# Conditioning weights as contiguous pieces with a third of their sums on TensorE, the memory projected token-major, six tiles begun by halves

## The reference

```
mod = silu(c) @ w_ada + b_ada            # c: 2048 numbers, w_ada: 2048 x 6144
shift, scale, gate = split(mod, 3)
h = rms(x) * norm_g * (1 + scale) + shift
proj = h @ w_in                          # 64 output tiles of 128 columns
```

```
m_k, m_v = split(rms(mem) @ w_mem_kv, 2)   # 2048 x 1024
kc = rms over each head of m_k; vc = m_v
oc = softmax(qc kc^T / sqrt(128)) vc * silu(c_gate)
```

## Time and profile before

| | |
|---|---|
| median of three runs | 2829.59 us |
| profiled execution | 2827.68 us, its span 2826.4 us |
| TensorE busy | 96%, weight loads 78% |
| VectorE, ScalarE, GpSimd busy | 38%, 37%, 46% |
| granted TensorE clock, mean | 0.979 |
| DMA | 323 MB, mean 114 GB/s |
| tenths of TensorE busy, first 4 of 40 slices (70.7 us each) | 7, 4, 7, 9 |
| its clock in these | 9, 6, 7, 9 |
| GB/s in these | 345, 262, 172, 209 |
| chain that ended last | TensorE 85%, VectorE 7%, GpSimd 3%, DMA 2% |

### The profile page before, as it was taken

How to read it: one execution, slowest core, us unless ns; L and a number is a source line. 1 busy time by engine, 2 the same in 40 slices (tenths; PEclk the granted TensorE clock), 3 DMA queues, 4 the chain that set the end, 5 groups by cost and what they waited for, 6 DMA issues and landing times.

```text
span 2826.4 us, 31555 instructions
## 1 busy us (share of the span) xinstructions
PE 2724.9 (96%) x12512; PEld 2203.1 (78%) x12512; DVE 1065.4 (38%) x1699; ACT 1059.1 (37%) x1744; POOL 1287.2 (46%) x647
## 2 busy tenths in 40 slices
PE   7479999999999999999999999999999999999999
PEld 5467788887877878878888777777888888888787
DVE  7867744334212212134467333333222222222300
ACT  5123333343433433234443444444444444333311
POOL 5664333333433335453334434444545555655543
PEclk9679999999999999999999999999999999999999
DMA  9745422122222223432222223222233333333343
GB/s 345 262 172 209 155 69 75 69 74 78 86 86 83 86 86 127 143 129 82 77 77 86 83 87 99 93 90 89 101 101 114 103 115 109 123 116 116 127 145 108
DMA packets 102963, 323.29 MB, mean 114 GB/s; under 512 B 11425, under 2 KB 14497, under 8 KB 102305
## 3 DMA queue, kind: packets, MB, share of 16 engines
q1 hardware_dynamic: 99072, 307.64, 31.5%
q10 hardware_dynamic: 3744, 13.63, 1.4%
HBM read 304.45 MB, written 16.78 MB: 114 GB/s over the span
## 4 chain that ended last, share of the span: by engine, by line
PE 85%; DVE 7%; POOL 3%; DMA 2%; issue 2%; ACT 2%; SPq 0%; DVEq 0%; ACTq 0%; POOLq 0%
PE bank L647 25%; PE bank L649 24%; PE bank L648 24%; PE bank L889 2%; PE bank L877 2%; DVE TA L1383 2%; POOL wlo L1763 2%; PE bank L808 2%; DVE TA L1583 1%; PE bank L869 1%; DMA TA<-in_strip 1%; PE bank L736 1%; ACT whi L946 1%; DVE Y L1383 1%; PE bank L839 1%
## 5 line engine op out<-in xcount | busy, mean ns | idle before, releaser
L1763 POOL TENSOR_TENSOR wlo<-wraw,whi 128x1024 fp32r<-128x1024 f32 (+2 forms) x454 | 1061.6, 2339 | 1346.5 <-ACT whi L946 1346.4
L647 PE MATMUL bank<-Hhi,whi 128*128 128x512 f32 x2928 | 1202.8, 411 | 20.0 <-POOL Hlo L1784 9.8
L648 PE MATMUL bank<-Hlo,whi 128*128 128x512 f32 (+1 forms) x3056 | 1190.2, 389 | 0.0
L649 PE MATMUL bank<-Hhi,wlo 128*128 128x512 f32 x2928 | 1150.7, 393 | 0.0
L946 ACT ACTIVATE whi<-wraw 128x1024 fp32r<-128x1024 f32 (+2 forms) x454 | 456.8, 1007 | 696.7 <-PE bank L649 695.5
L647 PEld LDWEIGHTS bank<-Hhi,whi 128*128 128x128 f32 x2928 | 554.6, 189 | 164.3 <-issue 31.6
L648 PEld LDWEIGHTS bank<-Hlo,whi 128*128 128x128 f32 x3056 | 584.5, 191 | 122.3 <-issue 14.0
L649 PEld LDWEIGHTS bank<-Hhi,wlo 128*128 128x128 f32 x2928 | 554.1, 189 | 120.1
L1383 DVE SCALAR_TENSOR_TENSOR TA<-TA,par 128x1024 f32<-128x1024 f32 x60 | 127.4, 2124 | 10.1 <-DMA TA<-in_w_ada 4.4
L647 PE MATMUL bank<-Ohi,whi 128*128 128x512 f32 x320 | 128.8, 403 | 0.0
L649 PE MATMUL bank<-Ohi,wlo 128*128 128x512 f32 x320 | 124.9, 390 | 0.0
(11 more groups left out here) (237 smaller groups left out, 2592.6 us busy)
## 6 DMA issues: line engine op xcount, KB each, us to landing
wraw<-in_w_in SPq DMA_DIRECT2D x304, 512.0 KB, 3.2
TA<-in_w_ada SPq DMA_DIRECT2D x64, 512.0 KB, 4.8
Y<-in_w_ada SPq DMA_DIRECT2D x32, 512.0 KB, 3.9
wraw<-in_w_out SPq DMA_DIRECT2D x32, 512.0 KB, 3.2
wraw<-in_w_o SPq DMA_DIRECT2D x32, 512.0 KB, 3.2
wraw<-in_w_mem ACTq DMA_DIRECT2D x16, 512.0 KB, 5.5
tmp_mgs<-TA SPq DMA_DIRECT2D x32, 256.0 KB, 2.0
TA<-tmp_mgs SPq DMA_DIRECT2D x32, 256.0 KB, 3.5
```

The source lines that it names most:

```text
L647: e.matmul(out, hi[:, c], xhi[k], start=first and j == 0, stop=False)
L648: e.matmul(out, hi[:, c], xlo[k], start=False, stop=False)
L649: m = e.matmul(out, lo[:, c], xhi[k], start=False, stop=last and end)
L1763: e.tensor_tensor(M.wlo[b][:, 0:w], M.wraw[b][:, 0:w], M.whi[b][:, 0:w].bitcast(F32), ALU.subtract).then_inc(S.lo)
```

## The change

- **Conditioning weights.** w_ada is laid out as 96 blocks of 128 x 1024, each contiguous. Of the first 64 pieces every third (`by_tensor`: a % 3 == 2, 21 of them) is taken by TensorE, eight one-column fp32 matmuls straight from the landed piece into the PSUM columns of the totals; VectorE sums the other 43, into one accumulator a chunk (two in turn), whose eight totals matmuls are added to the same columns. Six places instead of four. SP issues all 64 loads in its setup, x's loads among them, the masks' at the 40th. The chunks' order stays (2, 0, 3, 1).
- **Memory.** w_mem as 16 items of 128 features x 1024 columns, one a k. The memory tile is the stationary operand (128 tokens), the weights are the moving one, 512 wide: 12 matmuls a k into four banks, kept open over all k. The norm over features is a column per token: two one-column matmuls a k. Keys and values come out token-major, so values need no transpose; keys are normed by ScalarE's square, a reduce and a multiplication on VectorE (`mem_kv`) and turned by eight transposes on TensorE. Only tiles 0 to 7 are prepared in setup, 8 to 15 in the loop, whose steps also hold: x's squares and sums (k below 8), x's norm (k = 8 to 11), the gain and h tiles 0 to 7, two a step (k = 12 to 15), three conditioning pieces in each. The pair of the memory tiles lies behind HIGH of h.
- **Begun tiles.** The six are begun in another order and in other banks. Before each of the first four stand four conditioning pieces; before the sixth the totals of chunks 3 and 1 and the making of h tiles 8 to 15. The masks' cast follows them.
- **Gates.** One piece in three slots (`GATE_SLOTS`) instead of in each.

```diff
-BEGUN = (40, 32, 48, 56, 41, 33)
+BEGUN = (48, 33, 40, 32, 56, 41)
+
+CHUNKS = (2, 0, 3, 1)
+PLACES = 6
...
+def by_tensor(a):
+
+    return a % 3 == 2
+
+
+def taken(a, tensor):
+
+    return sum(by_tensor(i) == tensor for i in range(a + 1))
...
     do["setup"]()
-    beat.add("core", do["x_norm"]())
-    beat.add("slow", do["condition"]((2, 0), 0))
-    for h in range(4):
-        full("mem", "mem_k", h)
-        full("mem", "mem_v", h)
-    beat.drain("post", "core", "slow")
-    do["h_prep"](0)
-    beat.add("slow", do["condition"]((3, 1), 2))
+    for k in range(KT):
+        do["mem"](k)
+    beat.add("core", do["mem_kv"]())
 
 
     begun = {}
-    for tile, bank in zip(BEGUN, (beat.open(), beat.open(), BS0, BS1, BT, BST)):
+    for n, (tile, bank) in enumerate(zip(BEGUN, (BS0, BST, beat.open(), beat.open(), BS1, BT))):
         begun[tile] = bank
-        do["part"]("h", range(8), bank, True, False)
-    beat.drain("slow")
-    do["h_prep"](1)
+        if n < 4:
+            do["ada"](range(48 + 4 * n, 52 + 4 * n))
+        if n == 5:
+            do["h_gain"](1)
+            do["h_put"](HIGH)
+        do["part"]("h", LOW, bank, True, False)
+    beat.drain("core")
+    do["masks"]()
     beat.add("slow", do["gates"]())
...
+    def mem(k):
+
+        i = beat.item
+        hi, lo = M.whi[i % NRING], M.wlo[i % NRING]
+        xhi, xlo = M.pair["mem"]
+        pe.wait_ge(S.msq, k + 1)
+        for tt in range(2):
+            m = e.matmul(M.bST[:, tt:tt + 1], M.mem_sq[k % 8][:, tt * P:(tt + 1) * P], ones[:, 0:1],
+                         start=k == 0 and tt == 0, stop=k == KT - 1, skip_group_check=True)
+        m.then_inc(S.mst)
+        pe.wait_ge(S.lo, i + 1)
+        pe.wait_ge(*ready["mem", k])
+        for kv in range(2):
+            w = slice(kv * T, (kv + 1) * T)
+            for tt in range(2):
+                c, out = slice(tt * P, (tt + 1) * P), M.banks[MEM_BANKS[2 * kv + tt]]
+                e.matmul(out, xhi[k][:, c], hi[:, w], start=k == 0, stop=False)
+                e.matmul(out, xlo[k][:, c], hi[:, w], start=False, stop=False)
+                m = e.matmul(out, xhi[k][:, c], lo[:, w], start=False, stop=k == KT - 1)
+        m.then_inc(S.item)
+        if k < 8:
+            for x in (2 * k, 2 * k + 1):
+                pe.wait_ge(S.xsq, x + 1)
+                e.matmul(M.bS0, ones, M.xsq[x % 4], start=x == 0, stop=x == KT - 1).then_inc(S.xst)
+        ada(range(3 * k, 3 * k + 3))
+        if k == 6:
+            totals(0)
+        if k == 11:
+            totals(1)
+        if k >= 12:
+            h_put((2 * k - 24, 2 * k - 23))
+        beat.done("mem", [])
+        if k == KT - 1:
+            free[BS0], free[BST] = (S.xr, 1), (S.rr, 1)
+            free.update({bank: (S.mkv, n + 1) for n, bank in enumerate(MEM_BANKS)})
+            free[BVV] = (S.adp, 2)
+
+    def ada(pieces):
+
+        for a in pieces:
+            if by_tensor(a):
+                half, c = a // 32, a // 16 % 2
+                pe.wait_ge(S.ada[a % PLACES], 16 * (a // PLACES + 1))
+                pe.wait_ge(S.setv, 8)
+                for i in range(8):
+                    at = 8 * c + i
+                    m = e.matmul((M.bV, M.bO)[half][:, at:at + 1], M.ada_slot[a % PLACES][:, i * P:(i + 1) * P],
+                                 M.par[:, 64 + a % 16:65 + a % 16], start=a in (2, 32) and i == 0, stop=False,
+                                 skip_group_check=True)
+                m.then_inc(S.adq)
+
+    def totals(chunk):
+
+        pe.wait_ge(S.adm, taken(16 * chunk + 15, False))
+        for i in range(8):
+            at = 8 * (chunk % 2) + i
+            m = e.matmul((M.bV, M.bO)[chunk // 2][:, at:at + 1], M.ada_acc[chunk % 2][:, i * P:(i + 1) * P],
+                         ones[:, 0:1], start=False, stop=True, skip_group_check=True)
+        m.then_inc(S.adc)
+
+    def h_gain(half):
+        totals(2)
+        totals(3)
...
+    def mem(k):
+        if k < 8:
+            mem_gain(k + 8)
+        ada(range(3 * k, 3 * k + 3))
+        if k < 8:
+            mem_rest(k + 8)
+        elif k < 12:
+            for x in (4 * k - 31, 4 * k - 29):
+                dve.wait_ge(S.xr, 2)
+                e.tensor_tensor(M.y[x], M.y[x], M.xr, ALU.mult).then_inc(S.xnv)
+        else:
+            if k == 12:
+                h_gain(0)
+            h_put((2 * k - 24, 2 * k - 23))
+        beat.done("mem", [])
+
+    def ada(pieces):
+
+        for a in pieces:
+            if not by_tensor(a):
+                chunk, c, done = a // 16, M.par[:, 64 + a % 16:65 + a % 16], n.up("adm") - 1
+                acc, src = M.ada_acc[chunk % 2], M.ada_slot[a % PLACES]
+                dve.wait_ge(S.ada[a % PLACES], 16 * (a // PLACES + 1))
+                dve.wait_ge(S.setv, 8)
+                if done == taken(16 * chunk - 1, False):
+                    dve.wait_ge(S.adc, chunk - 1)
+                    e.tensor_scalar(acc, src, c, None, ALU.mult).then_inc(S.adm)
+                else:
+                    dve.wait_ge(S.adm, done)
+                    e.scalar_tensor_tensor(out=acc, in0=src, scalar=c, in1=acc, op0=ALU.mult,
+                                           op1=ALU.add).then_inc(S.adm)
+
...
+        for a in range(4 * 16):
+            if a in (0, 2, 4, 6):
+                i = a // 2
+                e.dma_start(M.Y[:, i * 2048:(i + 1) * 2048], io["xT"][:, i * 2048:(i + 1) * 2048]).then_inc(S.x[i], 16)
+            if a == 40:
+                e.dma_start(M.masks_in.bitcast(I32), io["masks"]).then_inc(S.mask, 16)
+            if a >= PLACES:
+                sp.wait_ge(S.adq if by_tensor(a) else S.adm, taken(a - PLACES, by_tensor(a)))
+            e.dma_start(M.ada_slot[a % PLACES], io["w_ada"][CHUNKS[a // 16], a % 16]).then_inc(S.ada[a % PLACES], 16)
...
-        "w_ada": I["w_ada"][0], "w_in": tiles(I["w_in"][0]), "w_out": tiles(np.roll(I["w_out"][0], 1024, axis=0)),
-        "w_mem": tiles(I["w_mem_kv_2"][0]), "w_in2": w_in2, "w_kv": w_kv,
+        "w_ada": I["w_ada"][0].reshape(128, 16, 6, 1024).transpose(2, 1, 0, 3), "w_in": tiles(I["w_in"][0]), "w_out": tiles(np.roll(I["w_out"][0], 1024, axis=0)),
+        "w_mem": I["w_mem_kv_2"][0].reshape(16, 128, 1024), "w_in2": w_in2, "w_kv": w_kv,
```

More of the change, by code:

```diff
@@ L978, in setup, with square @@
         load(NRING)
+        act.wait_ge(S.setv, 9)
+    def square(k):
+        act.wait_ge(S.mem[k // 4], 16)
+        act.wait_ge(S.mst, k - 7)
+        e.activation(M.mem_sq[k % 8], M.memt[k], ACT.Square).then_inc(S.msq)
+    def mem(k):
+        split(beat.item + 2)
+        load(beat.item + 4)
+        if k < 8:
+            square(k + 8)
+            for x in (2 * k, 2 * k + 1):
+                act.wait_ge(S.x[x // 4], 16)
+                act.wait_ge(S.xst, x - 3)
+                e.activation(M.xsq[x % 4], M.y[x], ACT.Square).then_inc(S.xsq)
+            put("mem", k + 8, M.memt, k + 8, ("mg", k + 9), None)
+        if k == 8:
+            act.wait_ge(S.xst, KT)
+            e.activation(M.xr, M.bS0, ACT.Ln, scale=1.0 / D, bias=M.eps).then_inc(S.xr)
+            act.wait_ge(S.xr, 1)
+            e.activation(M.xr, M.xr, ACT.Exp, scale=-0.5).then_inc(S.xr)
+        if k >= 12:
+            h_put((2 * k - 24, 2 * k - 23))
+        beat.done("mem", [])
@@ new lines, in h_gain @@
+    def h_gain(half):
+        dve.wait_ge(S.adc, 2 * half + 2)
+        for c in range(2):
+            cc = CHUNKS[2 * half + c]
+            e.tensor_tensor(M.par[:, 8 * cc:8 * cc + 8], (M.bV, M.bO)[half][:, 8 * c:8 * c + 8],
+                            M.c("b_ada", 8 * cc, 8), ALU.add).then_inc(S.adp)
+            n.up("adp")
+        dve.wait_ge(S.adp, n["adp"])
+        c = slice(16 + 8 * half, 24 + 8 * half)
+        e.tensor_scalar(M.par[:, c], M.par[:, c], 1.0, None, ALU.add).then_inc(S.vstep)
+        n.up("vstep")
+        step()
+        e.tensor_tensor(M.par[:, c], M.par[:, c], M.c("norm_g", 8 * half, 8), ALU.mult).then_inc(S.vstep)
+        n.up("vstep")
@@ L1389, in totals, with gates @@
-    def totals(chunks):
-        dve.wait_ge(S.adt, n.up("adt"))
-        for c, cc in enumerate(chunks):
-            e.tensor_tensor(M.par[:, 8 * cc:8 * cc + 8], M.bV[:, 8 * c:8 * c + 8], M.c("b_ada", 8 * cc, 8),
+    def gates():
+        for g in range(2):
+            for j in range(16):
+                i, done, c = 16 * g + j, n.up("adm") - 1, M.par[:, 64 + j:65 + j]
+                dve.wait_ge(S.adg[i % 3], 16 * (i // 3 + 1))
+                if j == 0:
+                    dve.wait_ge(S.adc, 4 + g)
+                    e.tensor_scalar(M.gate_acc, M.gate_slot[i % 3], c, None, ALU.mult).then_inc(S.adm)
+                else:
+                    dve.wait_ge(S.adm, done)
+                    e.scalar_tensor_tensor(out=M.gate_acc, in0=M.gate_slot[i % 3], scalar=c, in1=M.gate_acc,
+                                           op0=ALU.mult, op1=ALU.add).then_inc(S.adm)
+                yield from rest(GATE_SLOTS)
+            dve.wait_ge(S.adc, 5 + g)
+            cc = 4 + g
```

(1 more changed line is left out.)

407 lines of the change are left out of this document (179 added, 228 removed).

## The result

The kernel with the change takes 2796.26 us (median of four runs, 2792.75 to 2800.78), the one before 2828.96 in the same series: a ratio of 0.9886, interval [0.9867, 0.9905]. That is 32.7 us faster; 41 were forecast (29+12). The profiled execution took 2796.65 us (span 2795.3), 31.1 less in its span than before.

The account below looks back on a forecast made before the run. TensorE was taken as the bound, busy 2724.9 of 2826.4 us, its loss lying at the head. From 2827.7 us, 29 for the anchor and 12 for the gates were subtracted: 2786.7, predicted as 2787, range 2764 to 2812.

Parts of the forecast that it names:

- the anchor: End of the first part with HIGH on TensorE: forecast at 188 us instead of 217, 29 us gained.
- Step 2: Memory loop, k=0 to 7: 6.6 us a step on TensorE, but loads of 25.6 MB at 346 GB/s set 74 us.
- Steps 3 and 4: Memory loop, k=8 to 11 and 12 to 15: VectorE sets the pace, 31 and 29 us.
- The rival with that factor: VectorE and GpSimd fully block each other: loop steps of 9.1 and 8.2 us, 9 us more, 2796; chance 0.14.
- The 30% idleness of TensorE: Sign for the memory loop: between 74 and 133 us TensorE is idle about 30%, VectorE under 5%.
- The lockstep rival: Memory loop: each step's waits drop TensorE's clock; at 1.2 GHz throughout the kernel is at 2855 us; chance 0.08.
- Step 5: Begun tiles, pieces and totals between the memory loop's end and the anchor: 55 us, with VectorE's work and loads covered.
- Step 6: Conditioning pieces as contiguous blocks: no gain taken, since load rates were equal at 349 GB/s.
- loads gain: Rival: 12% more load rate cuts Step 2 from 74 to 70 us, some later pieces sooner, 2782; chance 0.12.
- Step 7: Gates at one sum in three slots: 12 us gained, bounds all 26.3 us back or a loss of 10.
- the sum of 153.8 us: TensorE's priced work from 217.0 to 397.1 us, half tiles and three chains; it took 180.1, so 26.3 lost.
- the lower bound: Step 7's worst case: a loss of 10 us, 32 gate sums meeting later chain steps at 0.3 us.

Follow-up runs that it names:

- e3: The changed kernel with gate sums in each slot again instead of every third: 2812.75 us, ratio 0.9954 to the kernel before.
- e14: The kernel before the change with only its gate sums respaced, one piece in three slots: 2812.21 us, ratio 0.9956 to the kernel before.
- e4: The changed kernel with only the first of the eight one-column products made in each TensorE conditioning piece: 2784.78 us, ratio 0.9851 to the kernel before.
- e11: The changed kernel with each TensorE conditioning piece as two 512-wide products, silu(c) column held, sums unused: 2794.44 us, ratio 0.9889 to the kernel before.
- e2: The changed kernel with every second conditioning piece on TensorE instead of every third: 2824.83 us, ratio 0.9998 to the kernel before.
- e8: The changed kernel with all of x's normalisation on VectorE, none on GpSimd, and h's gains on ScalarE: 2794.18 us, ratio 0.9883 to the kernel before.
- e1: The changed kernel with all 64 conditioning pieces summed on VectorE, none on TensorE: 2802.89 us, ratio 0.9915 to the kernel before.
- e5: The changed kernel with w_ada in its old layout, pieces as strided slices instead of contiguous blocks: 2799.01 us, ratio 0.9903 to the kernel before.
- e10: The changed kernel with every fourth conditioning piece on TensorE instead of every third: 2794.32 us, ratio 0.9883 to the kernel before.
- e12: The changed kernel with e11's wide products, x's normalisation all on VectorE and h's gains on ScalarE: 2790.27 us, ratio 0.9874 to the kernel before.

## Why the prediction was right, and where its sizes were not

Faster by over 0.3% was right, and 2796 lies in the range. The forecast of 2787 missed by 9.7 us, as two misses of opposite sign: 13 too much at the anchor, 3 to 5 too little for the gates (15.4 and 17.4 in the traces of e3 and e14).

**Step 2, 6 us short, and for another reason.** Step 7 was to end at 74 us by the loads; it ended at 80.1. Steps 0 to 2 take 9.6, 9.0 and 9.3 us instead of 6.6: the loads are full there, TensorE waits 2.6 us in all, and its clock is 0.81 and 0.82 in steps 1 and 2. From 43 us to the end of the loop TensorE waits for nothing and sets the pace itself: 6.7 us a step as priced, 8.5 in step 6 with the totals that I had left out, 8.3 in step 7 at clock 0.79. The loads' 346 GB/s of the earlier trace rows was what was asked for, not what could be had: 415 was measured above, and the kernel before itself moved 383 from 10 to 43 us. At 415 the 25.6 MB take 62 us. That TensorE sets the pace from 43 us on is shown by e4.

**Steps 3 and 4, right in size.** VectorE begins step 8's sums at 76.1 us and ends step 15 at 138.8, 62.7 us later (61 forecast with the root of x): 33.2 us for the four steps of normalisation (32), 29.5 for the four of gains (29). From 74 to 133 us it is idle 7.6% of the time (under 5% forecast). The sums cost 2.28 us beside GpSimd, as in the earlier trace rows. The price that I had a little too low is the normalisation, 1.87 us instead of 0.61+0.75x1.36 = 1.63. Counted as in the prediction, by GpSimd's prices alone (8x2.40+8x1.36 = 30.1 us, an estimate), 13 sums and 8 normalisations were slowed by 13x1.00+8x1.26 = 23 us, a factor of 0.77; beside GpSimd's busy 37.7 us it is 0.61. The Trainium skill's exclusive lock ("SBUF — State Buffer", section "SBUF: two separate sides") asks for a factor of 1; here it is below 1 by either count, so it again agrees in kind only. The rival with that factor forecast 2796, the measured time, but by chance: its steps were to take 9.1 and 8.2 us, and they took 8.3 and 7.4.

**The 30% idleness of TensorE, wrong.** From 43 to 133 us it is never idle. It fills the time by running slower: 0.82, then 0.72. From 80 to 133 us the mean is 0.77, and 53.0x0.77 = 41 us is what eight steps of 4.9 us and one totals of 1.8 cost at full clock: the 12 us between are the idleness that I had forecast. I had tied a low clock to waits, and took the four one-column groups of a step for harmless. e11 and e2 show that they are not: with the pieces as wide products the clock is 0.91 and 0.92, with half of the pieces on TensorE it is 0.69. The lockstep rival priced half clock throughout, 9.8 us a step; the steps took 6.6 on average, since the clock alternates between its two levels. TensorE left the loop as forecast (133.1 us, 133), which is luck: VectorE ended 3.8 us late, and TensorE was 5.7 us ahead of it instead of 2, which came back as the wait for piece 50.

**Step 5, the term that was mis-sized.** 55 us were forecast between the loop's end and the anchor; it took 67.6. Of the 12.6 us, 3.2 are the wait for piece 50, whose load stands in SP's queue behind one whose place VectorE had not freed; 1.7 that piece, at half clock; 5.2 the four tiles and tile five, nearly all at half clock in two places, 139.8 to 145 us and 159.4 to 164.6 (the second behind two pieces in a row); 1.6 tile six, where the clock falls again behind the totals' one-column products (7.0 us from 184.6 to 191.6, instead of 5.4); 0.6 the first part with HIGH. I had priced every tile at clock 1.00, out of a stretch where TensorE had long been busy with wide products. The price at clock 1.00 is not the only miss, though. e11 has a clock of 0.93 instead of 0.83 from piece 50 to the totals and takes the same 44.6 us, with 3.3 us of waiting for VectorE: the cover by VectorE that step 5 took for granted was gone as well. e8 shows the same on GpSimd's side: relief ahead of the totals is given back behind them, in part by GpSimd's remainders.

**Step 6, not refuted.** The layout was taken at nothing. In the traces it is about 3 us, in the time it can't be told from nothing, and where the DMA engines are full the rate is the same 415 GB/s. The "loads gain" rival had 12% more rate; it is 3.5% over 72 us.

**Step 7, right in kind, too small.** Gate spacing was to give 12 us with bounds of 26.3 and -10. Alone it gives 17.4 (e14), on top of the rest 15.4 (e3). Up to head 2 nearly all comes back (25.3 in e14, 24.7 with the change), but not all of it is won: about 11 us are waits, about 9 the clock (0.95 over 180 us), and 3.6 the two totals of the gates, which the sum of 153.8 us had left out and which only move behind head 2. There later heads pay 7.9 us (9.7 with the change), and not for the sums, as the lower bound had it: from head 3 to head 4 the change takes 57.2 us, with sums, as before without. What is paid lies at the first totals: 1.9 us of waiting, 2.7 for themselves and 2.3 for products at half clock behind them are 6.9 of the 7.1 us lost between heads 2 and 3, and the second totals (1.7 us at 554) are in the other 2.6, where behind head 3 nothing was to change. Half of the upper bound, as I took it, had no reason in the rows.

If the parts add, which no run tests, 15.9 us are all but the spacing, of which 7.2 are the third on TensorE (e1), 3.2 the layout (e5), and by difference 5.5 the memory projection, the places and the order of the tiles, which were not run alone. That the gain of the third is small fits bounds of nearly equal height, 133 us for TensorE and 139 for VectorE. A higher clock for TensorE alone (e11) or a quarter instead of a third (e10) gives nothing, relieving VectorE gives 3.0, and that with the higher clock (e12) 4.9.

What stays open: whether pieces as wide products, made to give their sums, would keep e12's gain (they need other room in PSUM); and why one-column products lower the clock.

## What to carry to other kernels

A step that never waits can still be slow: read the granted clock beside the idle time, and price work that follows a slow stretch or a wait at the clock that it leaves, not at that of a steady one. But look which engine stands next behind: here a higher clock alone gained nothing. Before moving work from one engine to another, put both engines' time for the step side by side; the best share is where they meet (a quarter to a third here), and beyond it the loss is steeper than the gain. Spreading background sums relieves the stretch that they leave; whatever hangs on their end, here the totals, is paid for in a later one, so measure both.

## What the runs showed of the hardware

- TensorE's granted clock fell to 0.72 from 106 to 133 us of the change, in steps in which it was never idle, 5.0 us long at full clock with 2.1 us of one-column fp32 products in each, and to 0.69 in e2 with half of the pieces on it. From 43 to 72 us, in steps of 6.7 us with two 512-wide fp32 statistics more, it stayed at 1.00. Waits lower it too: 0.67 from 72 to 106 us in e1, with 21 us of idleness.
- The same piece as two 512-wide products with one column held takes as long (1.88 us at the upper level) and kept the clock at 0.91 to 0.92 (e11, 72 to 133 us).
- A piece of eight one-column products took 1.84 us where the granted clock was 1.00 and 3.58 where it was 0.50; a wide product went from 0.227 to 0.43 us. Both double.
- Loads ran at 415 GB/s over 33 us, where the earlier trace rows had suggested a ceiling near 350. The rate was the same with contiguous pieces and with pieces at a pitch of 384 KiB (e5).
- Sixteen normalisations on VectorE cost it no more busy time than eight there with eight on GpSimd at once: from 72 to 106 us it is 31.5 us for 28 instructions against 31.3 for 19, with GpSimd's busy time down from 27.5 to 14.5.
